# Head norms in the first block: sums by column groups of TensorE, roots on a quarter of the columns, and new instruction sequences

## What is computed

```
def rms_norm(x, g):
    xf = x.astype(jnp.float32)
    y = xf * lax.rsqrt(jnp.mean(jnp.square(xf), axis=-1, keepdims=True) + NORM_EPS)
    return (y * g.astype(jnp.float32)).astype(x.dtype)

def l2_normalize(x):
    xf = x.astype(jnp.float32)
    return (xf * lax.rsqrt(jnp.sum(jnp.square(xf), axis=-1, keepdims=True) + 1e-6)).astype(x.dtype)
...
    q, k = l2_normalize(q), l2_normalize(k)                                    # GDN
    o = rms_norm(o, gdn_norm_g) * jax.nn.silu(z_b.reshape(bsz, s, h, GDN_HEAD_DIM))
...
    o = rms_norm(o, hgrn_norm_g) * jax.nn.silu(heads(z))                       # HGRN2
```

## Time and profile before

| | us |
|---|---|
| median of three runs | 1049.68 |
| lowest, highest | 1047.58, 1049.87 |
| span of the profiled execution | 1048.4 |
| PE busy | 1019.6 (97%) |
| DVE busy | 752.1 (72%) |
| ACT busy | 530.2 (51%) |
| chain that ended last: PE, DVE, ACT, DMA | 87%, 7%, 3%, 2% |
| mean granted PE clock | 0.994 |

### The profile page before, as it was taken

How to read it: one execution, slowest core, us unless ns; L and a number is a source line. 1 busy time by engine, 2 the same in 40 slices (tenths; PEclk the granted TensorE clock), 3 DMA queues, 4 the chain that set the end, 5 groups by cost and what they waited for, 6 DMA issues and landing times.

```text
span 1048.4 us, 21565 instructions
## 1 busy us (share of the span) xinstructions
PE 1019.6 (97%) x9120; PEld 897.6 (86%) x9120; DVE 752.1 (72%) x1049; ACT 530.2 (51%) x590; POOL 0.5 (0%) x7
## 2 busy tenths in 40 slices
PE   9999999999999999999999999989999999999998
PEld 7999999999866798989898787659986669999986
DVE  5999957678557668677787866867986775565553
ACT  5674544483353464435555433656687564335331
POOL 0000000000000000000000000000000000000000
PEclk8999999999999999999999999999999999999999
DMA  9454343244326664425343554876352446545441
GB/s 353 162 183 161 129 154 106 97 162 161 123 81 255 236 240 167 150 83 200 122 162 122 178 185 163 320 295 241 123 181 99 161 143 260 218 184 188 157 171 47
DMA packets 26302, 181.47 MB, mean 173 GB/s; under 512 B 3040, under 2 KB 3296, under 8 KB 4960
## 3 DMA queue, kind: packets, MB, share of 16 engines
q1 hardware_dynamic: 25056, 174.66, 45.2%
q10 hardware_dynamic: 1152, 5.45, 1.4%
HBM read 179.04 MB, written 1.05 MB: 172 GB/s over the span
## 4 chain that ended last, share of the span: by engine, by line
PE 87%; DVE 7%; ACT 3%; DMA 2%; issue 1%; SPq 0%; DVEq 0%; ACTq 0%
PE PS L916 84%; DVE WL L1799 2%; DMA RAW<-wst 1%; ACT WH L1386 1%; PE PS L1079 1%; DMA layer<-xt 1%; DVE X L1995 1%; DVE X L1996 1%; PE PS L1157 1%; PE PS L1307 0%; DVE STAT L1977 0%; DVE X L1976 0%; DVE layer_ln L2109 0%; DVE layer L2102 0%; ACT block L1690 0%
## 5 line engine op out<-in xcount | busy, mean ns | idle before, releaser
L916 PE MATMUL PS<-XTH,WH 128*128 128x256 f32 x1392 | 403.7, 290 | 6.2 <-issue 1.5
L916 PE MATMUL PS<-XTL,WH 128*128 128x256 f32 x1392 | 394.8, 284 | 0.0
L916 PE MATMUL PS<-XTH,WL 128*128 128x256 f32 x1392 | 394.7, 284 | 0.0
L1799 DVE TENSOR_TENSOR WL<-RAW,WH 128x2048 fp32r<-128x2048 f32 x138 | 314.2, 2277 | 99.8 <-ACT WH L1386 96.4
L1386 ACT ACTIVATE WH<-RAW 128x2048 fp32r<-128x2048 f32 x138 | 262.7, 1904 | 214.2 <-PE PS L916 208.7
L916 PEld LDWEIGHTS PS<-XTH,WH 128*128 128x128 f32 x1392 | 267.8, 192 | 12.6 <-issue 3.8
L916 PEld LDWEIGHTS PS<-XTL,WH 128*128 128x128 f32 x1392 | 268.0, 193 | 1.6 <-issue 1.4
L916 PEld LDWEIGHTS PS<-XTH,WL 128*128 128x128 f32 x1392 | 267.8, 192 | 0.0
L916 PE MATMUL PS<-WH,YH 128*128 128x512 f32 x224 | 89.6, 400 | 1.1 <-DVE YL L2274 1.1
L916 PE MATMUL PS<-WH,YL 128*128 128x512 f32 x224 | 87.4, 390 | 0.0
L916 PE MATMUL PS<-WL,YH 128*128 128x512 f32 x224 | 87.3, 390 | 0.0
(11 more groups left out here) (293 smaller groups left out, 1112.6 us busy)
## 6 DMA issues: line engine op xcount, KB each, us to landing
RAW<-wst SPq DMA_DIRECT2D x162, 1024.0 KB, 4.9
LNW<-lnrow ACTq DMA_DIRECT2D x3, 1024.0 KB, 6.7
RAW<-wst SPq DMA_DIRECT2D x4, 512.0 KB, 5.7
layer<-xt SPq DMA_DIRECT2D x2, 512.0 KB, 5.3
XR<-x ACTq DMA_DIRECT2D x1, 1024.0 KB, 4.7
out<-X SPq DMA_DIRECT2D x4, 256.0 KB, 3.3
CST<-cst ACTq DMA_DIRECT2D x1, 640.0 KB, 8.7
PT<-pt SPq DMA_DIRECT2D x1, 512.0 KB, 5.6
```

The source lines that it names most:

```text
L916: return pe.matmul(o, lhsT, rhs, start=start, stop=stop)
L1799: tt(WL[:, i % RAW_RING, 0:n], RAW[:, i % RAW_RING, 0:n], as_float(WH[:, k % SPLIT_RING, 0:n]), ALU.subtract).then_inc(vector_done, 1)
```

## The change

**q and k norms.** The sum of head h is made by the first 32 columns of ONES and written to the 32 partitions h*32 to h*32+31 of one bank: four matmuls of 32 output rows and 256 columns (`head_sums`). ACT and DVE then compute the root on 128 x 256 instead of 128 x 1024. A new step `spread` brings it back to 128 rows per head: four matmuls on 64 input rows each, whose stationary operand is one column of the identity repeated 128 times, into two banks. DVE then multiplies q or k with it (`v_spread`).

**Output norms.** The same sums (`gr`, `hr`), roots on 256 columns, then `grs`/`hrs`: four products on 32 input rows each, one for each of the banks 0 to 3 (`spread4`). ACT no longer copies the outputs, it only squares them, by halves of the tokens (`head_squares`); DVE reads them from PSUM as it applies gain and gate (`gq`, `hq`, before `gz`, `hz`). The last groups' sums are no longer cut in two; the final multiplication and split are (`gro`, `hro`). The buffers R2 and RF go.

**Waits.** ACT's `zb` and `z1` of the next group wait for `gq`/`hq` on DVE and no longer for the finished norm; ACT's squares of q wait for `spread` on PE; `pl` loses its wait for the last norm; `v_gc` loses its wait for `gr`.

**Sequences.** ORDER_T is new in most parts of the program, the second block too; ORDER_S and ORDER_V change only where the norms' steps do. Three places beside those shown below: in GDN a transposition `gx` that stood beside another one often stands alone now between the small products `gp` and `gu` (16 more changes between products of 64 output rows and whole ones, without the norms' steps); in the second HGRN2 group the step `first:f:2:1` comes five steps later; and where the first block ends, `ada:9:1 ada:4:0 adat:7 xt:4:1` has become `ada:9:1 adat:7 ada:4:0 xt:4:1`.

```
             def t_norm(step, kind, g):
                 pe.wait_ge(scalar_done, scalar_at(kind, g, 1))
-                for i in range(2):
-                    last = mm(PS[:, step.banks[i], :], ONES[:], SQ[:, i, :])
-                last.then_inc(tensor_done, 1)
+                head_sums(step.banks[0], lambda h: SQ[:, h // 2, h % 2 * T:(h % 2 + 1) * T]).then_inc(tensor_done, 1)
...
+            def head_sums(bank, squares):
+                for h in range(HG):
+                    last = mm(PS[h * QUAD:(h + 1) * QUAD, bank, 0:T], ONES[:, 0:QUAD], squares(h))
+                return last
+
+            def spread(o, roots):
+                for a in range(2):
+                    for b in range(2):
+                        r, s = slice(b * HD, (b + 1) * HD), b * HD + a * QUAD
+                        pick = ident[r, s:s + 1].to_broadcast([HD, P])
+                        last = mm(o(2 * b + a), pick, roots[r, :])
+                return last
+
+            def spread4(roots):
+                for h in range(HG):
+                    r = slice(h * QUAD, (h + 1) * QUAD)
+                    last = mm(PS[:, h, 0:T], ident[r, h * QUAD:h * QUAD + 1].to_broadcast([QUAD, P]), roots[r, :])
+                return last
...
             def s_norm(kind, g):
                 act.wait_ge(tensor_done, tensor_at("norm", kind, g))
-                b = bank_of("norm", kind, g)
-                rsqrt_and_square(flat(SQ), R2[:], PS[:, b:b + 2, :].rearrange("p b n -> p (b n)"), 1.0, 1).then_inc(scalar_done, 1)
+                rsqrt_and_square(NY, N2, PS[:, bank_of("norm", kind, g), 0:T], 1.0, 1).then_inc(scalar_done, 1)
...
+            def root(x, y, r2, to, scale, eps):
+                link(stt(x, x, eps / scale, r2, ALU.add, ALU.mult))
+                return stt(to, x, -1.5, y, ALU.add, ALU.mult)
...
+            def v_spread(kind, g):
+                dve.wait_ge(tensor_done, tensor_at("spread", kind, g))
+                to = tiles(KT if kind == "k" else QT0, g * HG, HG)
+                stt(to, to, -1.0, banks(bank_of("spread", kind, g), 2), ALU.mult, ALU.mult).then_inc(vector_done, 1)
...
             def s_pl(layer, n):
                 act.wait_ge(tensor_done, tensor_at("pl", layer, n))
-                act.wait_ge(vector_done, vector_at(*(("gr", 1, 1) if layer == 0 else ("hr", HGRN_GROUPS - 1, 1))))
...
 ORDER_T = """
...
-gv:1:1 go:1 gr:1:0 gr:1:1 pl:0:0 out:0:1:2 first:out:0:0:3 first:out:0:1:3 out:0:0:3 out:0:1:3 xt:0:0:0 pl:0:1 ada:0:0
+gs:1 gu:1:6:1 gks:1 out:0:0:2 gv:1:1 go:1 gr:1 grs:1 out:0:1:2 pl:0:0 first:out:0:0:3 first:out:0:1:3 out:0:0:3
...
-val:0:0 first:val:0:1 score:1 score:2 turn:0 val:0:1 first:val:1:0 turn:1 score:3 score:4 pv:0 pv:1 turn:2 val:1:0
+qn:1:0 feat:7 first:val:0:0 qn:1:1 score:0 val:0:0 score:2 first:val:0:1 turn:0 score:1 val:0:1 first:val:1:0 turn:1
+score:4 pv:0 score:3 turn:2 pv:1
```

More of the change, by code:

```diff
@@ L285, in gdn @@
                later(step, "gc2", g, on="V"),
-               later(step, "norm", "q", g, on="TSV", banks=(2, 3), readers="V"),
+               later(step, "norm", "q", g, on="TSV", banks=(2,), readers="V"),
+               later(step, "spread", "q", g, on="TV", banks=(2, 3), readers="V"),
                later(step, "vtr", g, on="TV", banks=(0, 1)),
@@ L513 @@
-ada:11:1 ff:0 adat:11 ff:1 ff:2 ff:3 ff:5 ff:4 ff:6 ff:8 ff:7 ff:9 ff:11 ff:10 ff:12 ff:13 ff:14 ff:15 ff:16 ff:17
-ff:18 ff:19 ff:21 ff:20 down:0:0 down:0:1 down:0:2 down:0:3 down:0:4 first:down:0:5 down:1:0 down:0:5 down:1:1
-down:1:2 down:1:3 down:1:4 first:down:1:5 down:1:5
+ba first:k:0:0 k:0:0 first:k:0:1 k:0:1 first:v:0:0 v:0:0 first:v:0:1 norm:k:0 first:q:0:0 v:0:1 gcc spread:k:0
+first:q:0:1 q:0:0 gc:0 q:0:1 first:zb:0:0 zb:0:0 first:zb:0:1 zb:0:1 first:k:1:0 k:1:0 norm:q:0 vtr:0 first:k:1:1 k:1:1
@@ new lines @@
+first:val:1:1 turn:6 score:9 pv:4 pv:5 score:10 turn:7 turn:8 pv:6 pv:7 score:11 ada:5:0 turn:9 score:12 pv:8 pv:9
+turn:10 score:13 mln turn:11 pv:10 ada:5:1 score:15 turn:12 pv:11 adat:5 turn:13 score:14 pv:12 pv:13 out2:0:0 turn:14
+out2:1:0 turn:15 pv:14 pv:15 first:out2:0:1 first:out2:1:1 out2:0:1 out2:1:1 ada:10:0 ada:10:1 ada:11:0 adat:10 xt:5:0
+xt:5:1 xt:5:2 xt:5:3 ada:11:1 ff:0 adat:11 ff:1 ff:2 ff:3 ff:5 ff:4 ff:6 ff:8 ff:7 ff:9 ff:11 ff:10 ff:12 ff:13 ff:14
+ff:15 ff:16 ff:17 ff:18 ff:19 ff:21 ff:20 down:0:0 down:0:1 down:0:2 down:0:3 down:0:4 down:0:5 first:down:0:5 down:1:0
@@ L516 @@
+down:1:1 down:1:2 down:1:3 down:1:4 first:down:1:5 down:1:5
 """
@@ L590 @@
+split:130:156 split:131:157 ff:20 split:132:158 ff:21 split:133:159 first:down:0:5 split:134:160 down:0:5 split:135:161
 split:136:162 split:137:163 split:138:164 first:down:1:5 down:1:5
@@ L793, in build @@
         HOT = A1.take(HG, T)
-        RF = tiles(FS, 0, HG)
         A2 = Arena("block2")
@@ L1027, in t_gk @@
             def t_gk(step, g):
-                pe.wait_ge(vector_done, vector_at("norm", "k", g))
+                pe.wait_ge(vector_done, vector_at("spread", "k", g))
                 for h in range(HG):
@@ L1033, in t_gkk @@
             def t_gkk(step, g):
-                pe.wait_ge(vector_done, vector_at("norm", "q", g))
+                pe.wait_ge(vector_done, vector_at("spread", "q", g))
                 for c in range(NT):
@@ L1110, in t_go, with t_gr, t_grs @@
                 last.then_inc(tensor_done, 1)
-            def t_gr(step, g, p):
-                pe.wait_ge(scalar_done, scalar_at("gq", g, p))
-                for i in dict(pieces(g, 2))[p]:
-                    last = mm(PS[:, 2 + i, :], ONES[:], tiles(SQO, 2 * i, 2))
-                last.then_inc(tensor_done, 1)
+            def t_gr(step, g):
+                for c in range(NT):
+                    pe.wait_ge(scalar_done, scalar_at("gq", g, c))
+                head_sums(2, lambda h: SQO[:, h, :]).then_inc(tensor_done, 1)
+            def t_grs(step, g):
+                pe.wait_ge(vector_done, vector_at("gr", g))
+                spread4(RO[:, 2, :]).then_inc(tensor_done, 1)
             def t_out(step, layer, n, part):
-                g, groups, name = (part, HGRN_GROUPS, "hr") if layer == 1 else (part - 2, 2, "gr")
+                g, groups, name = (part, HGRN_GROUPS, "hro") if layer == 1 else (part - 2, 2, "gro")
                 if g < 0:
@@ L1247, in t_ho, with t_hr, t_hrs @@
                 last.then_inc(tensor_done, 1)
-            def t_hr(step, g, p):
-                pe.wait_ge(scalar_done, scalar_at("hq", g, p))
-                for i in dict(pieces(g, HGRN_GROUPS))[p]:
-                    last = mm(PS[:, 2 + i, :], ONES[:], tiles(HS, 2 * i, 2))
-                last.then_inc(tensor_done, 1)
+            def t_hr(step, g):
+                for c in range(NT):
+                    pe.wait_ge(scalar_done, scalar_at("hq", g, c))
+                head_sums(2, lambda h: HS[:, h, :]).then_inc(tensor_done, 1)
+            def t_hrs(step, g):
+                pe.wait_ge(vector_done, vector_at("hr", g))
+                spread4(HS[:, 2, :]).then_inc(tensor_done, 1)
             def t_gates(step, part):
```

315 lines of the change are left out of this document (157 added, 158 removed).

## The result

| | kernel before | changed kernel |
|---|---|---|
| median, us | 1048.71 (4 runs) | 1061.20 (4 runs, 1060.99 to 1061.99) |
| ratio, 95% interval | | 1.0115 (1.0100 to 1.0129) |
| span of the profiled execution | 1048.4 | 1059.5 |

The change costs 12.5 us in the medians and 11.1 in the two profiled spans. 1059 was forecast.

A forecast was written before the change was run, and what follows sets the result against it. PE, busy 97% of the span, was taken to bound the kernel. Terms for norms, stall, clock, sequences and head loop summed to +9.2 on 1048.4, so 1057.6; the median, 1.3 above, gave 1059 us, eight-in-ten range 1046 to 1064.

The forecast's parts named there:

- The prices of the new steps: PE's cost in the new norms: `head_sums` 0.76 us, `spread` 1.24, `spread4` 0.82.
- the choice for the 32-row products: Output norms' spread on PE: four products run at once, 0.82 us; up to +6.9 in all if they do not overlap.
- third rival: 32-row products run one after the other (+7.7), or head loop absorbs nothing (+2.6): 1062 to 1067 us, chance 0.11.
- first rival: Only the array's time counts, its emptying hides and taken-apart scores are free: faster, about 1044 us, chance 0.15.
- The stall: GDN's end: PE waits for DVE's root ahead of the spread, +3.5 us, and half clock behind it, +1.7.
- The head loop: Second block: score pairs taken apart 7.2 us, `pv` pairs 1.7, 2.6 absorbed by waits, +6.3 (3 to 9).
- GDN's waves: `gcc` to `gr:1`: +2.2 us by the terms, including +1.0 for sixteen more changes between narrow and whole products.
- these waits I take as zero: PE's waits between sums and spread in the other nine norms: covered by 5.8 us or more of dense work.
- short waits of the same chain: GDN: sixteen more narrow/whole changes cost 2.6 us, part replacing such waits, so +1.0 (0 to 2.6).
- The bank wait of +0.5: HGRN2's second group: the step behind the spread waits for banks that DVE holds, +0.5 us.
- the removed waits: First block: PE's waits at 213.37 (0.78 us), 463.57 (1.25) and 478.14 (0.57) go behind dense work, -2.6.
- The block's end: First block's end: `adat:7` comes ahead, cuts PE's 3.04 us slab wait, clock may stay up, -1.6 us (-0.5 to -2.2).

The follow-up runs named there:

- Experiments 3 and 4: Changed kernel with the last GDN norm's spread behind a dense output-projection quarter: 1064.28 us; also with the old quarters one place later each: 1060.59 us.
- experiment 6: Changed kernel with the splits of slabs 37 and 38 exchanged on ACT and DVE, slab 38's subtraction behind the root: 1059.39 us, ratio 1.0096.
- experiment 2: Changed kernel with the old order of PE's steps from `feat:8` to the end: 1056.93 us, ratio 1.0073.
- experiment 7: Kernel before with `adat:7` moved ahead of `ada:4:0`: 1048.65 us; changed kernel with the old order of that pair: 1063.76 us.
- experiment 9: Kernel before with the 1 MB LNW load moved from `gate:1:1:1` to the copy of `ada:4:1`: 1046.57 us, ratio 0.9971.

## Why the prediction was right, and where it wasn't

- **The prices of the new steps** were right to 0.01: 0.76, 1.24 and 0.82 forecast, 0.77, 1.25 and 0.83 measured. They were built from neighbours (32 output rows from `ada`, 64 input rows from scores), and the choice for the 32-row products, four at once, was the right end of the range. So the third rival's first half falls, and so does the first rival: the emptying of the array doesn't hide.
- **The stall** was right in place, cause and size: 4.45 us idle (4.0 forecast), the clock at 0.50 behind it, +5.3 in the stretch (+5.2 for both terms). Experiments 3 and 4 show more than was claimed: with the work at hand it could be moved, but not filled; experiment 6 shortens it to 2.94.
- **The head loop** was right in its sum, +6.30, and in its main step: a single score costs nearly what a pair costs. That the sum came out to the tenth is luck. The prediction counted 7.2 for the scores, 1.7 for `pv` and took 2.6 off for waits that the added work would replace. By the same sums as in experiment 2 the scores cost 5.6 more (0.80 a pair and not 1.03), and all the rest 0.7, where 1.7 - 2.6 = -0.9 were counted: dense work 0.4, `pv` and the transpositions 0.3 each, the other steps and the waits 0.3 less. The waits that PE's rows show in the loop are 1.78 before and 1.69 after, so 0.1 of them was replaced.
- **GDN's waves** were mis-sized. From `gcc` to `gr:1` +4.3 came, where the terms give +2.2. The spread of k and the norms are 1.25 + 0.9 - 0.1 = 2.05 of it. The new waits of the changed kernel, less the one removed, are 0.59 + 0.37 - 0.78 = 0.2:

```profile
71.85 0.84 PE L1053 MATMUL PS<-CST,layer 128*128 128x128 f32 x6 [0.59 <-ACT layer L1479]
79.03 1.14 PE L920 MATMUL PS<-layer,CST 64*128 64x256 f32 x8 [0.37 <-DVE layer L1798]
```

  The first is a wait that the shorter sums laid bare: they end 0.9 us earlier, and the transposition behind them still needs ACT's copy. The second contradicts "these waits I take as zero". The remaining 2.0 are left for the sixteen more changes between narrow and whole products, where the prediction took 1.0 of 0 to 2.6. A level of the second wave (one round of its `gp`, `gx` and `gu` steps) with a pair of transpositions in the kernel before, and the same with single ones in the changed kernel:

```profile
274.45 0.69 PE L916 MATMUL PS<-layer,layer_x 128*64 128x64 f32 x16 [0.17 <-DVE layer L1921]
277.92 0.69 PE L916 MATMUL PS<-layer,layer_x 128*64 128x64 f32 x16 [0.17 <-DVE layer L1921]
279.05 1.09 PE L1079 MATMUL PS<-CST,layer_x 128*128 128x128 f32 x8
280.07 0.69 PE L916 MATMUL PS<-layer_x,layer 128*64 128x64 f32 x16
```

```profile
276.68 0.69 PE L920 MATMUL PS<-layer,layer_x 128*64 128x64 f32 x16 [0.18 <-issue]
277.29 0.66 PE L1108 MATMUL PS<-CST,layer_x 128*128 128x128 f32 x4
277.88 0.69 PE L920 MATMUL PS<-layer_x,layer 128*64 128x64 f32 x16
280.41 0.69 PE L920 MATMUL PS<-layer,layer_x 128*64 128x64 f32 x16 [0.18 <-issue]
```

  A pair of transpositions costs 1.02, a single 0.59. The level lasts 3.73 (276.68 to 280.41) where it lasted 3.47 (274.45 to 277.92), 0.26 more, with one more excursion between narrow and whole products in it and the same short wait of 0.17 or 0.18 ahead. Eight such excursions are 2.1, an estimate that accounts for the 2.0. So the price per excursion was near (0.33 forecast), and the discount for "short waits of the same chain" was the error: the waits are as long as before.
- **HGRN2** was mis-sized too: -0.1 and not -1.8. The bank wait of +0.5 came as 0.39. Of the removed waits, those at 213.37 and 463.57 went, the one at 478.14 did not (0.57 at 486.96), and one more came elsewhere (0.64 at 475.42). (`adat:3` now waits 1.73 at 608.81, but before it waited 0.85 there and a step just ahead of it 0.95.) All in all PE is idle for 0.8 us less than before in this stretch, and 0.7 of work were added, where 0.4 less were forecast. Most of that has a place that neither the description of the change nor the prediction has: four pairs of `ada` steps in the tails of the two layers (1, 2, 8 and 6) stand side by side before and apart after. A pair passes in 1.86, a single in 1.00 (597.55 to 598.55), so at least 0.6 for the four, and up to 1.3 by the 0.33 for each further excursion; this is an estimate, and no run puts these pairs back. A wait that is covered in one place is not a gain until one has looked at what comes next, and a moved step has a price too.
- **The block's end** was right in sign and nearly in size (-2.2, forecast -1.6) for a wrong reason. The failed step is "Now `adat:7` comes ahead and falls into that wait and cuts it": experiment 7 gives 0.3 for it, and the clock fell all the same. In the kernel before it was LNW's load beside the slab's that made the wait (experiment 9); that the two meet otherwise in the changed kernel is the likely reason for its gain, and not shown. I had taken the 3.04 as given and never asked what else the DMA engines were moving.
- **Not forecast:** -1.2 ahead of the head loop (a wait of 1.22 for ACT's copy of a slab, gone with the new order) and -0.4 at the end.

The errors are +2.1 and +1.7 on one side, -0.6, -1.2 and -0.4 on the other, beside those that cancel inside the head loop: 1059 for 1061.2 is close partly by luck.

## What to carry to other kernels

A step that is split in two, with another engine's work between, brought two waits here, one for the result and one for the banks until they are read; count the pieces of independent work at hand, and at a layer's end there may be one too few. Two scores on the two halves of the rows cost what one costs, and two transpositions side by side 1.02 and not 2 x 0.59, so price a new sequence by how many neighbours it parts, and list all of them. And where an engine waits for a load, look at what the other queues asked for in the same microsecond: moving one early 1 MB load was worth more here than any of the norms' arithmetic.
